# QKV and gate units of a gated mLSTM and attention layer moved between stages, GpSimd square sums and low parts, attention's low keys on 128 rows

## The reference

```python
z = rmsnorm(x, g_mix) @ w_in          # mq mk mv mo mi mf fq fk fv ff ga gb
h  = mlstm(mq, mk, mv, mi, mf)        # 4 heads of 128, chunks of 128, carried state
y  = forgetting_attention(rmsnorm(fq), rmsnorm(fk), fv, ff)   # 8 heads of 64
a  = (rmsnorm(h) * sigmoid(mo)) @ w_pa
b  = y @ w_pb
x  = x + (sigmoid(ga) * a + sigmoid(gb) * b) @ w_out
gu = rmsnorm(x, g_ffn) @ w_gu
x  = x + (silu(gu[:, :D_FF]) * gu[:, D_FF:]) @ w_down         # D_FF = 2816
x  = x + sigmoid(rmsnorm(x, g_ple) @ w_ple_gate) * (p @ w_ple_proj)
```

## Time and profile before

| what | before |
|---|---|
| median of 3 runs | 2348.0 us (2345.8 to 2350.44) |
| profiled execution, its own time | 2341.82 us |
| its span | 2340.2 us |
| mean granted TensorE clock | 0.946 of full speed |
| PE busy | 2082.0 us, 89% |
| DVE, ACT, POOL busy | 886.7, 534.1, 575.8 us (38%, 23%, 25%) |
| longest waits of PE, whole run | 39.9 us for `xn` (5 times), 27.6 us for `kpg` (2), 23.7 us for `XR` (20) |

### The profile page before, as it was taken

The page is one execution under the profiler, slowest core; times in us unless marked ns, Lnnn a source line. Parts: engine busy times, 40 slices in busy tenths (PEclk is TensorE's granted clock), DMA queues, the critical chain, the costliest instruction groups (busy, mean ns, idle before and its releaser), DMA issues.

```text
span 2340.2 us, 33231 instructions
## 1 busy us (share of the span) xinstructions
PE 2082.0 (89%) x12507; PEld 1902.8 (81%) x12507; DVE 886.7 (38%) x1525; ACT 534.1 (23%) x845; POOL 575.8 (25%) x391
## 2 busy tenths in 40 slices
PE   2999997999968988947788999999999999998888
PEld 2877776999957777734687989999999999998688
DVE  4500001323346666642374323443344433444433
ACT  5212112221144454411532220011000110001311
POOL 0312222111122131100222242323223232320521
PEclk9999998998989898967899999999999999999999
DMA  3222215443222222146632121111111111100121
GB/s 120 68 80 108 88 43 165 131 138 114 76 55 77 63 72 63 49 157 217 206 117 64 36 72 37 44 46 42 47 36 54 36 54 36 45 27 27 48 71 37
DMA packets 203827, 179.44 MB, mean 77 GB/s; under 512 B 49114, under 2 KB 168126, under 8 KB 203746
## 3 DMA queue, kind: packets, MB, share of 16 engines
q1 hardware_dynamic: 154594, 151.28, 20.5%
q10 hardware_dynamic: 48160, 27.40, 3.9%
q0 software_dynamic: 1024, 0.13, 0.1%
HBM read 141.68 MB, written 39.26 MB: 77 GB/s over the span
## 4 chain that ended last, share of the span: by engine, by line
PE 76%; DVE 8%; issue 7%; ACT 2%; DMA 2%; POOL 2%; SPq 1%; ACTq 1%; DVEq 0%; POOLq 0%
PE pair L2164 23%; PE bank L2164 19%; PE bank L1860 9%; PE bank L1887 7%; PE pair L1860 4%; PE pair L2001 2%; PE pair L1975 1%; DVE dd L1475 1%; PE pair L1985 1%; PE pair L1974 1%; DVE ptl L1522 1%; PE pair L2054 1%; POOL tmp L949 1%; PE pair L1963 1%; DVE XR L1789 1%
## 5 line engine op out<-in xcount | busy, mean ns | idle before, releaser
L2164 PE MATMUL bank<-acth,wha 128*128 128x352 f32 x640 | 213.3, 333 | 30.0 <-DVE actl L1683 17.1
L2164 PE MATMUL bank<-actl,wha 128*128 128x352 f32 x640 | 210.5, 329 | 0.0
L2164 PE MATMUL bank<-acth,wla 128*128 128x352 f32 x640 | 210.5, 329 | 0.0
L2164 PE MATMUL pair<-hh,whb 128*128 128x352 f32 x528 | 173.5, 329 | 24.2 <-DVE XR L1789 23.7
L915 POOL CAST wha<-raw 128x1024 fp32r<-128x1024 f32 x46 | 52.1, 1132 | 523.2 <-PE pair L2164 190.5
L1887 PE MATMUL bank<-acth,fwh 128*128 128x352 f32 x480 | 172.2, 359 | 3.4 <-POOL fwl L835 3.4
L2164 PE MATMUL pair<-hl,whb 128*128 128x352 f32 x528 | 169.2, 320 | 0.0
L2164 PE MATMUL pair<-hh,wlb 128*128 128x352 f32 x528 | 169.2, 320 | 0.0
L1789 DVE TENSOR_TENSOR XR<-XR,pair 128x352 f32<-128x352 f32 x264 | 134.2, 518 | 81.4 <-PE pair L2164 81.2
L1887 PE MATMUL bank<-actl,fwh 128*128 128x352 f32 x480 | 165.0, 344 | 0.0
L1887 PE MATMUL bank<-acth,fwl 128*128 128x352 f32 x480 | 164.5, 343 | 0.0
(11 more groups left out here) (422 smaller groups left out, 5066.9 us busy)
## 6 DMA issues: line engine op xcount, KB each, us to landing
raw<-in_w_gu SPq DMA_DIRECT2D x44, 512.0 KB, 3.9
wraw<-in_w_in SPq DMA_DIRECT2D x24, 512.0 KB, 4.8
scratch_zA<-stage SPq DMA_DIRECT2D x48, 256.0 KB, 2.0
raw<-in_w_down SPq DMA_DIRECT2D x22, 512.0 KB, 3.3
scratch_zT<-fout ACTq DMA_DIRECT2D x20, 528.0 KB, 2.7
fraw<-in_w_in SPq DMA_DIRECT2D x20, 512.0 KB, 4.3
gs<-scratch_zT SPq DMA_DIRECT2D x16, 528.0 KB, 3.5
kpg<-in_cache_k SPq DMA_DIRECT2D x32, 256.0 KB, 4.8
```

The costliest lines, as they stand in the source:

```text
L2164: ins = nc.tensor.matmul(out, w[i](k), x[j](k), start=n == 0, stop=n == total - 1)
```

## The change

1. Phase 1 keeps three QKV groups (MG = 3). The 27 units of fq, fk, fv become `f_unit`, 7, 7, 7 and 6 of them in the four mLSTM heads, where the gate units stood. The first two are issued before the phase's barrier, the third right behind it. The weights go through a ring of 5 slots, and POOL makes both the cast and the subtraction of the last eight pieces (`split_unit_weights(4)` to `(11)`).
2. All 60 gate units move to attention: 4 ahead of head 0 and 7 in each head, in halves. Their weights have two buffers instead of three. SP instead of ACT stores the results to `zT`.
3. `klo` has 128 rows: the second logit matmul contracts over 128 rows like the first, which adds the product of the low parts.
4. Before the FFN and in the PLE stage POOL adds up squares elementwise in `rv` (ACT squares in both), and PE sums over partitions at the end: three pairs of matmuls instead of 30 before the FFN; in the PLE stage one pair each for two column tiles and eight for the third.
5. In the FFN POOL instead of DVE makes the low parts (`low_hidden`), DVE does the last `unit_hidden` behind the first residual addition, and POOL's list of pieces has a new order.
6. The PLE stage loads `pin` early and begins its casts, squares and low parts inside the last FFN group; its products start ahead of the sums.
7. The loops of phases 1 to 3 are written out.

```diff
+RING = 5
+MG = 3
+UNITS = 27
+PRE = 4
+NGATE = 60
...
-        klo = take("klo", [DH, SEQ], F32R)
+        klo = take("klo", [P, SEQ], F32R)
...
+            for g in range(HM):
+                for u in range(7 * g, min(7 * g + 7, UNITS)):
+                    store_f(u)
+                    if u in (0, 10, 12, 14):
+                        load_piece1({0: 8, 10: 9, 12: 10, 14: 11}[u])
+                    if u % 7 == 4 and g < HM - 1:
+                        load_qk(g + 1)
+                if g < HM - 1:
+                    load_v(g + 1)
+                    load_rows(g + 1)
...
+            for g in range(HF):
+                for u in range(PRE + 7 * g if g else 0, PRE + 7 * g + 7):
+                    if u % 3 == 2:
+                        store_gate(u // 3)
+                        if u // 3 + 3 < NGATE // 3:
+                            load_gate(u // 3 + 3)
+                    if u == PRE + 7 * g + 4 and g:
+                        store_y(g - 1)
+                if g < HF - 1:
+                    load_row(g + 1)
+            store_y(HF - 1)
...
+            def split_unit_weights(n):
+
+                q, j = MG + n // PIECES, n % PIECES
+                hi, lo = piece_parts(q, j)
+                pool.wait_ge(w_in1[j], 16 * (q + 1))
+                old = n - RING
+                if old >= 0 and old % PIECES < PIECES - 1:
+                    pool.wait_ge(w2_free, old // PIECES * (PIECES - 1) + old % PIECES + 1)
+                elif old >= 0:
+                    pool.wait_ge(fu_mm, (old // PIECES + 1) * XTILES)
+                nc.gpsimd.tensor_copy(hi, wraw[:, j]).then_inc(pool_own2, 1)
+                pool.wait_ge(pool_own2, n - 3)
+                nc.gpsimd.tensor_tensor(lo, wraw[:, j], hi.bitcast(F32), ALU.subtract).then_inc(w_lo1, 1)
...
+            def low_hidden(g, j):
+                for t in range(NT):
+                    pool.wait_ge(h_hi, g * 6 + 3 * j + t + 1)
+                    nc.gpsimd.tensor_tensor(hl[:, j, t * TW:(t + 1) * TW], un[:, (3 * j + t) % 2, :], hh[:, j, t * TW:(t + 1) * TW].bitcast(F32),
+                                            ALU.subtract).then_inc(h_lo, 1)
+
+            ffn_pieces(0, 0)
+            with pool.Fori(0, NFF // 2 - 1) as g:
+                ffn_pieces(g, 2)
+                ffn_pieces(g, 4)
+                low_hidden(g, 0)
+                ffn_pieces(g + 1, 0)
+                low_hidden(g, 1)
...
-                    ins = nc.tensor.matmul(out[:, c:c + w], q[0:DH, :], klo[:, c:c + w], start=False, stop=not last)
+                    ins = nc.tensor.matmul(out[:, c:c + w], q, klo[:, c:c + w], start=False, stop=not last)
...
-                    if u == 3:
-                        sums(0)
-                sums(1)
+            pe.wait_ge(xg_lo, 3 * KC)
             for t in range(NT):
-                nc.tensor.matmul(BANK[4 + t][:, 0:TW], ones[:], rv[:, t, :], start=False, stop=True).then_inc(ss5_mm, 1)
+                pe.wait_ge(sq5_add, 3 + 3 * KC - NT + t + 1)
+                nc.tensor.matmul(BANK[4 + t][:, 0:TW], ones[:], rv[:, t, :], start=True, stop=True).then_inc(ss5_mm, 1)
```

More of the change, by code:

```diff
@@ L99, in program @@
         phase_base = top[0]
+        ring = take("ring", [P, RING, 2, 2, W], F32R)
+        ring_end = top[0]
+        wraw = take("wraw", [P, 4, 2, W])
+        stage = take("stage", [P, 3, W])
+        attn_base = top[0]
+        wh1 = take("wh1", [P, KC, W], F32R)
+        wl1 = take("wl1", [P, KC, W], F32R)
+        rows_base = top[0]
         xt = take("xt", [P, 2, D])
@@ L109, in program @@
         p1_small = top[0]
-        top[0] = phase_base
+        top[0] = rows_base
         gx = take("gx", [GW, T])
@@ L130, in program @@
         assert top[0] <= ROOM, top[0]
[L133 to L138, removed]
+        top[0] = ring_end - 4 * W * 4
+        ms_row = take("ms_row", [HM, T])
+        assert top[0] <= ring_end
+        top[0] = attn_base
         q_in = take("q_in", [P, NCH + 1, DM])
@@ L252, in program @@
         pjl = take("pjl", [P, 2, 2, P], F32R)
+        pin = at("pin", top[0], [P, NCH + 1, PLE])
         yst7 = take("yst7", [P, 2, NCH + 1, P])
@@ L643, in load_head @@
[L643 to L652, removed]
@@ L845, in pool_mlstm @@
                 nc.gpsimd.tensor_tensor(rB8, rB8, gcur[:, 0:NCH].unsqueeze(2).to_broadcast([P, NCH, P]), ALU.add).then_inc(rm_done, 1)
[L846 to L854, removed]
+            pool_mlstm(0)
+            split_unit_weights(4)
+            pool_mlstm(1)
+            for n in range(5, 9):
+                split_unit_weights(n)
+            pool_mlstm(2)
+            for n in range(9, 12):
+                split_unit_weights(n)
+            pool_mlstm(3)
             end_phase(pool)
@@ L2004, in values3, with gate_half, gate @@
                 ins.then_inc(pv_mm, 1)
+            def gate_half(u, half):
+                c, t = u // 3, u % 3
+                if half == 0:
+                    if t == 0:
+                        pe.wait_ge(f_lo, c + 1)
+                    if u >= 2:
+                        pe.wait_ge(f_out, u - 1)
+                n = 12 * half
+                for k in range(4 * half, 4 * half + 4):
+                    for w, x in ((fwh, acth), (fwh, actl), (fwl, acth)):
+                        ins = nc.tensor.matmul(BANK[u % 2][:, 0:TW], w[:, c % 2, k, :], x[:, k, t * TW:(t + 1) * TW],
+                                               start=n == 0, stop=n == 3 * KC - 1)
+                        n += 1
+                if half:
+                    ins.then_inc(f_mm, 1)
+            def gate(h):
+                gate_half(h // 2, h % 2)
             def pe_head(g):
-                gate = lambda f, half: gate_unit(g, f, 1, HM, half)
+                h = 2 * (PRE + 7 * g)
                 turn3(g)
-                gate(0, 0)
+                gate(h)
+                gate(h + 1)
                 pe.wait_ge(qk_lo, g + 1)
@@ new lines, in square_sums @@
+            def square_sums(t):
+                if t < 2:
+                    pe.wait_ge(sq7_add, (t + 1) * (KC - 1))
+                    nc.tensor.matmul(BANK[4 + t][:, 0:TW], ones[:], rv[:, t, :], start=True, stop=True).then_inc(ss7_mm, 1)
+                    return
+                for c in range(KC):
+                    pe.wait_ge(sq7, 2 * KC + c + 1)
+                    nc.tensor.matmul(BANK[6][:, 0:TW], ones[:], sqt[:, (2 * (KC - 1) + c) % 3, :], start=c == 0, stop=c == KC - 1).then_inc(ss7_mm, 1)
```

678 lines of the change are left out of this document (368 added, 310 removed).

## The result

The changed kernel took 2207.94 us (median of 4 runs, 2204.28 to 2212.81), the kernel before 2346.9 us in the same comparison (4 runs, 2338.74 to 2350.44): a ratio of 0.9414, 95% interval 0.9383 to 0.9445. The forecast was 2208, 2165 to 2258. Part of that closeness is luck: by the two traces the change is 2211.1 - 2340.2 = -129.1 us, not -137; the profiled execution of before lay 5 us under its median and that of after 5 us above.

The account below looks back on a forecast made before the run. TensorE, busy for 89% of the span, bounds the kernel. Phases 1 to 3 -78, w_out -19, FFN -23, PLE -17 make -137: 2341.8 becomes 2204.8, and half the profiled run's distance to the median gives 2208; range 2165 to 2258.

Parts of the forecast that it names:

- QKV units out of phase 1: Phase 1: 27 units of 5.56 us leave, making the phase 150 us shorter.
- mLSTM heads: mLSTM stage: gate units leave, QKV units come in, weights wait 11 us; last update ends at 507, -127 us.
- rival of a clock that recovers everywhere: Whole kernel: mLSTM gains 12 us, the y store costs nothing, attention falls some 8 us further: 2178; chance 0.17.
- Attention: Attention: turn into it -2 us; heads 47.0 us each if the clock recovers, +41; y store wait +10.
- The rival of chain-bound heads: Attention heads: producers' waits stay and the clock stays at 0.92, 53.4 us a head: 2259; chance 0.17.
- The y store: Attention heads 3 and 6: a gate store ahead of the y store delays DVE, 5 us each, +10.
- w_out: w_out stage: sums of squares leave PE, POOL's last six additions cost about 1.3 us: -19 us.
- FFN: FFN: un*gn and hl go from ahead of the additions, ending the XR waits of 2.4 us a group: -23.
- The rival of the shared port: FFN: the gap stays since POOL's subtractions hold DVE at another place: +23, 2231; chance 0.10.
- PLE: PLE stage: pin and POOL's squares leave the path, the norm factor's wait of about 7.7 us comes: -17.
- Slower: FFN: POOL paces the groups, each losing 14.0 us, 154 in all: 2382; chance 0.03.

Follow-up runs that it names:

- the run without it: The changed kernel with the store of the previous head's y ahead of the gate store in SP's list: 2188.25 us, ratio 0.9331.
- the two runs above: The changed kernel, 2207.94 us, and the changed kernel with the y store ahead of the gate store, 2188.25 us.
- the late VectorE version: The changed kernel with the FFN's low parts on VectorE, the last two behind the fifth and eleventh residual additions: 2214.36 us, ratio 0.9434.

## Why the prediction was right, point by point

The total is closer than its parts. Attention and w_out came out 9 and 5.5 us worse than the forecast, the FFN and the PLE stage 5 and 2 us better, so that part of the misses cancel.

- **QKV units out of phase 1** and **mLSTM heads**: -148.9 and an update that ends at 506.8 (forecast 507). The waits for the ring were 10.7 us where 11 were taken. That the weight waits behind POOL's row additions is shown by the run that reversed them: only the place of the wait changed. The wait for `qs` in head 0, 7.0 us, was not in the sum, whose 3 us for the pace of ACT and SP stood in part for it. The rival of a clock that recovers everywhere failed in this stage, at 0.90 against 0.89.
- **Attention.** The price of the low keys, 0.33 us a pair and 4.0 a head, came out as 3.85, and the head at 45.8 to 48.2 us where 47.0 was taken "if the clock recovers": it did, 1.00 against 0.92. The run with three units per head shows that the filled waits are the larger part, 67 us; the prediction had them as 3.75 us of waits and the clock's 2.8, 6.5 us a head, 52 in all. Its 30.0 us of waits left out the 4.7 at L1985. The rival of chain-bound heads is refuted for seven units; with three the waits and the lower clock are there.
- **The y store** was seen with its place, its heads and its chain, and undersized: 5 us each were taken, and the run without it gave 19.7 us, 17.2 of them in these two heads. The clock's fall behind the wait (0.94 and 0.91) is in that. With it goes a smaller error: the eight heads of before took 332.3 us, not 8 x 41.93 = 335.4. Together they make +59.7 of the forecast +51.
- **w_out**: the stretch gave 13.5 us, undoing it cost 16.7; 19 was too much. The 16.6 us of busy time of the pairs was taken whole, but these spans overlap those of the products beside them: from the first to the last w_out product it was 106.4 us and is 94.4, so only 12.0 left the path. The end of the stage grew more than the 1.3 us: the FFN's first product came 9.7 us behind the last w_out product, where it was 7.9.
- **FFN**: right in the cause, the additions held up by what stands ahead of them on VectorE while GpSimd subtracts. Both un*gn and hl were said to matter; the run with hl back and un*gn moved lost everything, the run with hl later regained most of it. So hl is shown to matter; for un*gn it is not shown, since no run leaves it alone ahead of the additions. The size was read from the waits (2.4 us a group) and is 3.24, since 0.1615 us a matmul held part of the start; back to back they are 30.52 / 192 = 0.159. The last group gave 5.0 us back (its last addition ends at 2048.84, 73.6 us behind that of the group before; the kernel before had 68.7 there): its additions share VectorE with the low parts of the PLE stage and come 1.19 us apart instead of 0.95.
- **The rival of the shared port** didn't come about as a longer gap. The Trainium skill (SBUF — State Buffer, section "SBUF: two separate sides") states that a VectorE instruction with two SBUF inputs and a GpSimd one that reads SBUF exclude each other, and the traces agree: hl of 2.26 us beside a subtraction of 2.53, where it took 0.52 with GpSimd idle; kws of 3.35 beside a subtraction of 3.23, which took 2.37 by itself. What it cost depended on what stood behind: no wait of PE in the first ten FFN groups of the changed kernel.
- **PLE**: -19.2, 17 taken. **Slower**: POOL had 294 us of work in 755 us of FFN, and behind the FFN's first product no wait of PE there names it.

## What to carry to other kernels

A filler unit is worth what it covers: the same 32 units cost 67 us when they stood in a row instead of in the waits, and a saving of TensorE work in a stage bound by a chain (the low keys alone: 14 of 31 us) comes in full only after the waits are filled. When a store is moved to another queue, look at which later instruction needs that queue's next entry: one swapped line was worth 20 us. And before work is moved to another engine, try it later on the same one: its place in the list, beside GpSimd's subtractions, was worth 28 of 34.5 us.

## What was not expected of the hardware

One wait of 6.8 us in an otherwise filled head went with a granted clock of 0.94 for that head, against 1.00 in its neighbours, so a wait costs more than its length: heads 3 and 6 lost 8.4 and 8.8 us to it. In head 3, 6.3 us of that is time in which PE stood idle, and 2.2 us is the same matmuls taking longer (47.79 us busy against 45.63, in the windows of the two runs above). What the low parts' engine itself is worth stays open: the late VectorE version is 6 us behind the changed kernel, within the intervals, and its groups are 0.87 us longer, but its low parts stand at other places too.
